# Attention heads in pairs: the 64-row score products issued two at a time, the 64-column value products by query block and in turn

## The reference, cut to what matters

```python
def mla_attention(...):       # first block, 8 heads; scores contract 64+32 features, values 64 wide
    s = (jnp.einsum('bqhd,bkhd->bhqk', qn, k_nope)
         + jnp.einsum('bqhr,bkr->bhqk', qr, k_r)).astype(jnp.float32) * scale
    probs = jax.nn.softmax(s, axis=-1).astype(v.dtype)
    return jnp.einsum('bhqk,bkhd->bqhd', probs, v)

def windowed_gqa(...):        # first block, 8 query heads on 2 key heads, 64 wide, a window of 128 keys each way
    s = jnp.einsum('bnqhgd,bnkhd->bnhgqk', q, kw).astype(jnp.float32) * scale
    s = s - slopes[...] * dist[...]                  # and a mask
    m = jnp.maximum(jnp.max(s, axis=-1, keepdims=True), sink_l)
    e = jnp.exp(s - m)
    probs = (e / (jnp.sum(e, axis=-1, keepdims=True) + jnp.exp(sink_l - m))).astype(v.dtype)
    o = jnp.einsum('bnhgqk,bnkhd->bnqhgd', probs, vw)

def dsa_attention(...):       # second block, 8 heads on one key head, 64 wide, causal, only the selected keys
```

## Time and profile before

| | us |
|---|---|
| median of 3 runs | 3031.95 (3026.61 to 3032.58) |
| profiled execution, its own time | 3030.81 |
| its span, first to last instruction | 3029.0 |
| mean granted TensorE clock | 0.977 of 2.4 GHz |
| PE busy | 2875.7 (95%) |
| DVE busy | 1492.7 (49%) |
| ACT busy | 1082.7 (36%) |

### The profile page before, as it was taken

The page is one execution under the profiler, slowest core; times in us unless marked ns, Lnnn a source line. Parts: engine busy times, 40 slices in busy tenths (PEclk is TensorE's granted clock), DMA queues, the critical chain, the costliest instruction groups (busy, mean ns, idle before and its releaser), DMA issues. The chain is left out here.

```text
span 3029.0 us, 36528 instructions
## 1 busy us (share of the span) xinstructions
PE 2875.7 (95%) x13124; PEld 2264.2 (75%) x13124; DVE 1492.7 (49%) x2287; ACT 1082.7 (36%) x1711; POOL 446.3 (15%) x319
## 2 busy tenths in 40 slices
PE   5999999999999899999999999989999999899998
PEld 4885567888887688556788888767677578688886
DVE  4347684543324534668453332455578635543323
ACT  3335433422224433443343222343533334532221
POOL 1010011211102301001131111230011113211101
PEclk9999999999999999999999999999998899999999
DMA  3221012222232122101222223222222122122232
GB/s 114 97 98 56 15 56 84 70 97 97 97 111 93 69 98 86 68 15 43 84 84 87 96 96 110 98 70 84 84 97 84 42 70 84 42 84 97 97 110 85
DMA packets 37056, 245.92 MB, mean 81 GB/s; under 512 B 4144, under 2 KB 5168, under 8 KB 7984
## 3 DMA queue, kind: packets, MB, share of 16 engines
q1 hardware_dynamic: 33600, 239.09, 22.6%
q10 hardware_dynamic: 3312, 4.93, 0.5%
HBM read 241.91 MB, written 2.10 MB: 81 GB/s over the span
## 5 line engine op out<-in xcount | busy, mean ns | idle before, releaser
L524 PE MATMUL bank<-h_hi,w_hi 128*128 128x512 f32 (+1 forms) x2280 | 883.5, 387 | 21.4 <-DVE w_lo L1409 10.6
L526 PE MATMUL bank<-h_hi,w_lo 128*128 128x512 f32 (+1 forms) x2280 | 865.3, 380 | 0.0
L525 PE MATMUL bank<-h_lo,w_hi 128*128 128x512 f32 (+1 forms) x2280 | 865.1, 379 | 0.0
L1409 DVE TENSOR_TENSOR w_lo<-raw,w_hi 128x2048 fp32r<-128x2048 f32 x225 | 519.7, 2310 | 555.5 <-ACT w_hi L970 396.5
L524 PEld LDWEIGHTS bank<-h_hi,w_hi 128*128 128x128 f32 x2280 | 432.0, 189 | 117.5 <-issue 30.4
L526 PEld LDWEIGHTS bank<-h_hi,w_lo 128*128 128x128 f32 x2280 | 432.1, 190 | 81.3
L525 PEld LDWEIGHTS bank<-h_lo,w_hi 128*128 128x128 f32 x2280 | 432.6, 190 | 80.0 <-issue 3.4
L970 ACT ACTIVATE w_hi<-raw 128x2048 fp32r<-128x2048 f32 x143 | 273.3, 1911 | 307.5 <-PE bank L526 297.5
L524 PE MATMUL bank<-a_hi,w_hi 128*128 128x512 f32 x528 | 205.4, 389 | 0.0
L525 PE MATMUL bank<-a_lo,w_hi 128*128 128x512 f32 x528 | 205.4, 389 | 0.0
L526 PE MATMUL bank<-a_hi,w_lo 128*128 128x512 f32 x528 | 205.4, 389 | 0.0
(11 more groups left out here) (368 smaller groups left out, 4149.8 us busy)
## 6 DMA issues: line engine op xcount, KB each, us to landing
raw<-in_stream SPq DMA_DIRECT2D x226, 1024.0 KB, 4.9
x<-in_xT SPq DMA_DIRECT2D x2, 1024.0 KB, 12.7
out_T<-x ACTq DMA_DIRECT2D x8, 256.0 KB, 2.1
p_f<-in_pT ACTq DMA_DIRECT2D x2, 512.0 KB, 3.8
memf<-in_memT ACTq DMA_DIRECT2D x1, 1024.0 KB, 5.2
cst_sb<-in_cst ACTq DMA_DIRECT2D x1, 411.5 KB, 6.8
pos_i<-in_pos ACTq DMA_DIRECT2D x1, 258.0 KB, 9.4
vec<-in_vec ACTq DMA_DIRECT2D x2, 26.0 KB, 1.8
```

What stands on the lines that cost most here:

```text
L524: nc.tensor.matmul(ps, wh, xh, start=start, stop=False)
L525: nc.tensor.matmul(ps, wh, xl, start=False, stop=False)
L526: return nc.tensor.matmul(ps, wl, xh, start=False, stop=stop)
L1409: nc.vector.tensor_tensor(w_lo[s][:, :], raw[s][:, :], w_hi[s][:, :].bitcast(F32), ALU.subtract).then_inc(lo_ready, 1)
```

## The change

The items of a stage with `per_tile=2` are counted in another order, by pair of heads, then query block, then head: `items_of` gives head 0 block 0, head 1 block 0, head 0 block 1, and so on. All three engines use it.

In `gqa` and `dsa` (the stages with `biased=True`) PE issues two score products together at every even t, one on partitions 0 to 63 and one on 64 to 127, and waits before them for `shift_ready` of item t-1 in place of `exp_done` of item t-2. In `mla` a score product is issued in every turn as before.

The value products of a head are no longer made at one go. After every second item, `values_of_pair` makes those of one query block for both heads: matmuls 128 queries wide, one of the even head and one of the odd head in turn. There are 16 such groups in a stage in place of 8. ACT copies the high part of a finished pair after the transposes of the second item of the next pair (turn 8p+4 for the pair p-1), DVE the low part in turn 8p+5, ahead of the scaling, and PE needs it for the first value product of pair p, which it reaches in turn 8p+5.

```diff
-    stage("z1b", A=1, HP=1), stage("mla", I=32, H=8, O=4), stage("gqa", I=32, H=8, O=4),
+    stage("z1b", A=1, HP=1), stage("mla", I=32, H=16, O=4), stage("gqa", I=32, H=16, O=4),
...
+        def items_of(a):
+
+            if a["per_tile"] == 2:
+                return [(2 * pair + one, b) for pair in range(a["heads"] // 2) for b in range(ST) for one in range(2)]
+            return [(h, b) for h in range(a["heads"]) for b in range(ST)]
...
+                def scores(t):
+                    h, b = items[t]
+                    ks = a["keys"](b)
+                    nc.tensor.matmul(SCORES[t % 2][:, 0:len(ks) * P], a["q"](h, b), a["k"](h, ks),
+                                     start=True, stop=True).then_inc(logits_done, 1)
                 for t in range(len(items) + LAG):
-                    if t < len(items):
-                        h, b = items[t]
+                    if t < len(items) and a["biased"]:
+                        if t % 2 == 0:
+                            if t >= 2:
+                                pe.wait_ge(shift_ready, c.at("I", st, t))
+                            scores(t)
+                            scores(t + 1)
+                    elif t < len(items):
                         if t >= 2:
                             pe.wait_ge(exp_done, c.at("I", st, t - 1))
-                        ks = a["keys"](b)
-                        nc.tensor.matmul(SCORES[t % 2][:, 0:len(ks) * P], a["q"](h, b), a["k"](h, ks),
-                                         start=True, stop=True).then_inc(logits_done, 1)
+                        scores(t)
...
-                        if b == ST - 1 and h >= 1:
+                        if a["per_tile"] == 2:
+                            if i >= 2 and i % 2 == 0:
+                                values_of_pair(c, st, i // 2 - 1)
+                        elif b == ST - 1 and h >= 1:
                             values(c, st, h - 1)
...
+            def values_of_pair(c, st, q):
+
+                a = ATT[st]
+                pair, b = q // ST, q % ST
+                pe.wait_ge(turn_taken, c.at("I", st, 2 * q + 2))
+                if b == 0 and (pair >= 1 or st != "mla"):
+                    pe.wait_ge(o_split, c.at("O", st, pair))
+                ks, at = a["keys"](b), slice(b * P, b * P + P)
+                for j, t in enumerate(ks):
+                    for one in range(2):
+                        mm = nc.tensor.matmul(VALUES[64 * one:64 * one + 64, at], a["v"](2 * pair + one, t), a["pT"][one][:, j, at],
+                                              start=j == 0, stop=j == len(ks) - 1)
+                mm.then_inc(head_done, 1)
...
-                        if h >= 2 and b == 0:
+                        if a["per_tile"] == 2 and h >= 2:
+                            act.wait_ge(head_done, c.at("H", st, ST * (h // 2 - 1) + b + 1))
+                        elif a["per_tile"] == 1 and h >= 2 and b == 0:
                             act.wait_ge(head_done, c.at("H", st, h - 1))
...
-                        if b == ST - 1 and h >= 1 and h % a["per_tile"] == 0:
-                            output_hi(c, st, h // a["per_tile"] - 1)
+                        if a["per_tile"] == 2 and b == 0 and h % 2 == 1 and h >= 3:
+                            output_hi(c, st, h // 2 - 1)
+                        elif a["per_tile"] == 1 and b == ST - 1 and h >= 1:
+                            output_hi(c, st, h - 1)
...
+                    if a["per_tile"] == 2 and t % 8 == 5 and 13 <= t < len(items):
+                        output_lo(c, st, taken)
+                        taken += 1
...
-                        if b == 2 and h >= 2 and (h + 1) % a["per_tile"] == 0 and (h + 1) // a["per_tile"] >= 2:
-                            done = (h - 1) // a["per_tile"]
-                            while taken < done:
-                                output_lo(c, st, taken)
-                                taken += 1
+                        if a["per_tile"] == 1 and b == 2 and h >= 2:
+                            output_lo(c, st, taken)
+                            taken += 1
```

More of the change, by code:

```diff
@@ L178 @@
     stage("bm2", A=8), stage("am", A=8), stage("normm", R=8, SQ=8, SS=8, N=1),
-    stage("mk", A=4, HP=1), stage("mv", A=2, HP=1), stage("dsa", I=32, H=8, O=4), stage("cm", A=8, R=8),
+    stage("mk", A=4, HP=1), stage("mv", A=2, HP=1), stage("dsa", I=32, H=16, O=4), stage("cm", A=8, R=8),
     stage("wout", A=8, SS=6, AD=7), stage("post1", N=2, X=16),
@@ L647, in attention @@
                 a = ATT[st]
-                items = [(h, b) for h in range(a["heads"]) for b in range(ST)]
+                items = items_of(a)
                 for sem_, value in ready:
                     pe.wait_ge(sem_, value)
-                for t in range(len(items) + LAG):
-                    if t < len(items):
-                        h, b = items[t]
+                def scores(t):
[3 more added lines that the diff above has]
+                                     start=True, stop=True).then_inc(logits_done, 1)
+                for t in range(len(items) + LAG):
+                    if t < len(items) and a["biased"]:
[5 more added lines that the diff above has]
+                    elif t < len(items):
                         if t >= 2:
                             pe.wait_ge(exp_done, c.at("I", st, t - 1))
-                        ks = a["keys"](b)
-                        nc.tensor.matmul(SCORES[t % 2][:, 0:len(ks) * P], a["q"](h, b), a["k"](h, ks),
-                                         start=True, stop=True).then_inc(logits_done, 1)
+                        scores(t)
                     if t >= LAG:
@@ L673, in attention @@
                         also(t)
-                values(c, st, a["heads"] - 1)
+                if a["per_tile"] == 2:
+                    values_of_pair(c, st, len(items) // 2 - 1)
+                else:
+                    values(c, st, a["heads"] - 1)
+            def values_of_pair(c, st, q):
[10 more added lines that the diff above has]
+                mm.then_inc(head_done, 1)
@@ L676, in values @@
             def values(c, st, h):
                 a = ATT[st]
-                per = a["per_tile"]
                 pe.wait_ge(turn_taken, c.at("I", st, ST * h + ST))
[L681 to L698, removed]
@@ L699, in values @@
+                pe.wait_ge(o_split, c.at("O", st, h))
+                n = len(a["keys"](0))
+                for t in range(n):
+                    mm = nc.tensor.matmul(VALUES[:, :], a["v"](h, t), a["pT"][h % 2][:, t, :], start=t == 0, stop=t == n - 1)
                 mm.then_inc(head_done, 1)
@@ L1136, in output_hi @@
                 a = ATT[st]
-                act.wait_ge(head_done, c.at("H", st, (i + 1) * a["per_tile"]))
+                act.wait_ge(head_done, c.at("H", st, (i + 1) * (ST if a["per_tile"] == 2 else 1)))
                 nc.scalar.activation(a["o"](i)[0], VALUES[:, :], ACT.Copy).then_inc(o_hi_ready, 1)
```

## The result

The changed kernel takes 3011.84 us (median, 3009.25 to 3013.64); the kernel before, on the same chip, 3031.91 us (3026.61 to 3032.58). The ratio is 0.9938, with a 95% interval of 0.9923 to 0.9953: faster by 20 us. The forecast was 2990 us, 41 us faster; the direction and the range of 2966 to 3018 held, the gain was half of the one forecast. The profiled execution took 3011.73 us, with a span of 3009.6 us.

What follows compares the result with a forecast made beforehand. PE was taken to bound gqa and mla, and dsa in part, with DVE 2.3 us behind in gqa. Gains of 17 (mla), 18 (gqa) and 6 (dsa), 41 us from 3030.8, gave 2990 us; range 2975 to 3005, wider 2966 to 3018.

Steps and rivals of the forecast that it cites:

- Score products in pairs: In gqa and dsa, the second product of 64 rows is free beside the first: 11.8 us a stage.
- Value products in turn: Two heads' value products for the price of one; a group takes 1.10 us in mla, 0.9 in gqa and dsa.
- The short windows: Trace windows at mla's end: sixteen passes in 5.42 us, eight in 3.65; 0.064 against 0.11 us a pass.
- The wait that is added: PE waits for DVE's low part three times a stage: 1.5 us in mla, 2.5 in gqa, 2.0 in dsa.
- my upper bound of 4: Bound on each low-part wait: about 4 us, were a 3.6 us split of POOL in DVE's way.
- The sum: Stage gains: mla -8.4 and gqa -9, each twice, dsa -6 after +3 for its clock; 41 us in all.
- the 2 given back: In gqa, 2 us taken off the 10.9 us gain for uneven turns, PE and DVE being so near each other.
- The rival that put `gqa` at 0.77: PE's holes at every pair lower gqa's clock, about 26 us more a stage; 3042 us, chance 0.06.
- the list of what would show the forecast wrong: Value groups of 1.9 us in mla; PE waiting for DVE's shift at most even turns; gqa's clock under 0.95.
- DVE takes most of it: New pair wait and low part put DVE in PE's path: mla -5, gqa -3, dsa -2; 3013 us, chance 0.25.

Runs made afterwards that it cites:

- e3: Changed kernel, but in gqa and dsa both score products of a pair use partitions 0 to 63; 3019.82 us.
- e1: Changed kernel, but the first value group of the second, third and fourth pair is issued one group later, directly ahead of the pair's second; 2969.17 us.
- e5: e1, but both heads' value products go to columns 0 to 63 and one half of the bank, one head after the other; 3006.58 us.
- e6: e1, each head on its own columns, but the even head's value products of a group all issued before the odd head's; 2983.78 us.
- e2: Changed kernel, but DVE takes the low part in turn 8p+4 behind the scaling, ahead of the gating and the split; 2987.77 us.
- e8: e1, but PE's score pair waits only until DVE's bias operation has read the bank, not for the shift; 2950.97 us.
- e7: e1, but gqa and dsa issue one score product a turn, behind the exponential of item t-2; 2985.31 us.

## Why the prediction was half right

**Score products in pairs: right.** "The second is free": 0.92 us for four records of 384 columns, and 0.63 us more when both products use the same rows (e3).

**Value products in turn: right.** 1.10 us a group was forecast for `mla`, 1.09 measured, 1.96 without the sharing (e5). PE's saving in the first `gqa` was forecast as 10.9 + 7.5 = 18.4 us before waits; e1's busy time, at the same clock of 1.00, is 123.08 - 103.46 = 19.6 us below that of before. The sixteen passes at the end of `mla` were read as an overlap although one head's were issued first; e6 has that order, and its overlap is the weaker one. The short windows gave the right price.

**"The wait that is added": this step failed, in its size.** It priced each wait at 1.5 us in `mla`, 2.5 in `gqa` and 2.0 in `dsa`; measured are 5.1 / 3 = 1.7, 14.2 / 3 = 4.7 and 10.8 / 3 = 3.6, and the longest, 5.4, lies above my upper bound of 4. PE came when it was forecast to, 373.15 - 369.46 = 3.7 us behind the start of the pair's score products (forecast 3.6). DVE came late: it was done with the low part at 378.5, 9.0 us behind that start, where the sum had 6.1. Its way was counted as "one item (13.1 / 4 = 3.3 us), half of the next and 0.68", which spreads the gating and the split, 1.4 + 2.29 us, evenly over the items. Turn 8p+4, ahead of the very item that the low part follows, took 376.27 - 370.40 = 5.9 us in place of 3.3, with both in it. The second wait, with the gating alone there, was 3.3 us, still above the 2.5. e2 moves only DVE's place for the low part and takes 11 of the 14 us of this wait away; e1 takes the wait away and gains 43 us.

**The clock had no price in `mla` and `gqa`: this step failed too.** The sum gave it 3 us, in `dsa` alone. Taken apart, the first `gqa` has 19.6 us saved on PE, 6.9 given back by the clock (110.39 - 103.46 for the same matmuls) and 16.8 given back as time without work (19.9 - 3.1): 4.1 longer, where -9 was forecast. Against the terms of the forecast that is 1.2 us more saved, 7.3 more without work (the waits' 7.5 and the 2 given back make 9.5) and 6.9 for the clock, which had none. For `mla` at a clock of 1.00 there is e8:

```profile
237.66:323.46 85.80, 79.67 (x521) 51.56 (x521) 58.67 (x140) 46.17 (x105) 7.20 (x2) 1.00 0.11 38
```

89.92 - 79.67 = 10.3 us saved (12.9 forecast before waits), 82.62 - 79.67 = 3.0 given back by the clock and 9.2 - 6.1 = 3.1 as time without work: -4.2 for a forecast of -8.4. Only part of the 3.0 us belongs to the new wait. A stretch at the low clock near 246 us, behind a wait of 2.6 us for ACT that the kernel before has as well, is in e1's `mla` too, where nothing waits for the low part:

```profile
240.14:328.87 88.73, 82.61 (x520) 52.99 (x520) 58.69 (x140) 46.22 (x105) 7.20 (x2) 0.96 0.10 37
```

The rival that put `gqa` at 0.77 and the kernel at 3042 us was too strong (by its own terms even 113 / 0.77 = 147 us a `gqa`, 34 more and not 26), but its mechanism acts, at 0.93 and 0.92, and a clock under 0.95 in `gqa` was on the list of what would show the forecast wrong. I had argued against it from `mla`'s holes of 0.4 and 2.3 us; these are sums over 19 and 11 us, and those that the change makes in `gqa` are 3.3 to 5.4 us each.

**`dsa` was underrated**, -10.8 for -6. PE's busy time fell there by 25.4 us, with the granted clock at 0.85 for 0.78 in place of the loss I had written down; by e7 the score pairs bring the most in this stage, in part through the clock. This hid some of what `gqa` lost: the total came into the range by errors that partly cancel, and 3.8 of the 19.4 us lie outside the stages, by chance.

**The rival "DVE takes most of it"** named 3013 us, 1 us from the result, with `mla` at -5, `gqa` at -3 and `dsa` at -2; measured are -4.2 and -5.8, +4.1 and +1.1, and -10.8. The total agrees by chance, the parts don't. It named the low part and the shift as what comes into PE's path, and e1, e2 and e8 bear that out. Its ground, that DVE has only 2.3 us of 15.42 to give, they don't: DVE is busy for 97.8 us in the changed kernel's `gqa` and for 98.0 in e8's, which is 19.5 us shorter. DVE had the time, at another place in its order. (By rows 1 it had 27 to 45 us to spare in the three windows and not 20 to 45; nothing rests on this.)

Open: why the clock falls at one wait and not at another. In `mla` one wait of 2.8 us came with this, in the 13 us around it in the changed kernel:

```profile
281.00:294.00 13.00, 11.28 (x74) 6.92 (x75) 9.81 (x23) 6.13 (x15) 0.00 (x0) 0.87 0.23 82
```

The first `gqa` of e1, whose longest wait is 2.8 us too, stays at 1.00. Its second `gqa`, with the same waits, doesn't:

```profile
1297.51:1415.87 118.36, 106.49 (x593) 76.08 (x593) 98.59 (x248) 46.36 (x140) 21.49 (x6) 0.97 0.13 45
```

So a wait of this length brought the fall in one layer and not in the other. The clock's share of e1's gain differs from stage to stage: read as the difference of PE's busy time it is 6.9 of 15.1 us in the first `gqa`, 4.1 of 12.1 in the second, 3.0 of 6.1 in the second `mla` and none of 3.1 in the first, where e1 has 0.96 itself, and 4.7 of 9.1 in `dsa`.

## What to carry to other kernels

When a change makes one engine wait for another at a fixed turn, write down what the other has to do up to exactly that point, operation by operation: a mean per item hid 1.4 us of gating at all three places in `gqa`, and at two of them a 2.3 us operation beside it. Then ask whether the waiting work can be issued a step later, which here was worth twice the change itself (e1), and whether the signal comes as soon as the buffer is read (e8). The price of such an edit belongs to the order around it: the shorter wait was worth 18 us on e1 and some 4 without it, and the earlier low part gained 24 us on the changed kernel and lost 27 on e8.

## What the runs showed of the hardware

- Two series of value products for different 64 columns share the array best when they are issued in turn: sixteen passes of 128 columns took 1.09 us in turn, 1.58 one series after the other, 1.96 on the same columns.
- In the first `gqa` of the changed kernel the second and third wait of PE for the low part, 3.3 and 5.4 us, were followed by 4 to 5 us at a granted clock of 0.50 with PE busy throughout, so such a wait is paid for a second time: the same 593 records took 110.4 us in place of 103.5.
- Shorter waits were followed by it only at times: e1's two `gqa` have the same waits, the longest 2.8 us, and a granted clock of 1.00 and of 0.97.
